# Where ScalarE rounds the fourth seam block's weights: ahead of or behind two low masks

## What is computed

```python
def ssd_chunked(x, dt, a, bm, cm):          # 4 chunks of 128 tokens, 4 groups of 8 heads
    ...
    a_cum = jnp.cumsum(a_dt, axis=-1)
    decay_mat = jnp.exp(segsum(a_dt))
    cb = jnp.einsum('bclgn,bcsgn->bgcls', cm, bm)
    y_diag = jnp.einsum('bgecls,bcsgep->bclgep', cb[:, :, None] * decay_mat, xdt)
    ...
    y_off = jnp.einsum('bclgn,bcgepn,bgecl->bclgep', cm, prev, jnp.exp(a_cum))
    return (y_diag + y_off).reshape(b, s, SSM_HEADS, SSM_HEAD_DIM)
```

## Time and profile before

| | us |
|---|---|
| median of 3 runs | 1220.28 (1220.24 to 1220.58) |
| the profiled execution, whole | 1220.1 |
| its span, first to last instruction | 1218.4 |
| TensorE busy in it | 1203.7 (99%) |
| VectorE busy | 856.1 (70%) |
| ScalarE busy | 641.1 (53%) |
| GpSimd busy | 88.6 (7%) |

### The profile page before, as it was taken

One profiled execution on the slowest core, in us unless ns is written; L12 is line 12 of the kernel. 1 busy time (PEld: TensorE's weight loads), 2 busy tenths in 40 slices (PEclk: granted clock), 3 DMA queues, 4 the chain that ended last, 5 costly groups with the idle time before them and its releaser, 6 DMA issues.

```text
span 1218.4 us, 16218 instructions
## 1 busy us (share of the span) xinstructions
PE 1203.7 (99%) x5941; PEld 1005.8 (83%) x5941; DVE 856.1 (70%) x1573; ACT 641.1 (53%) x1193; POOL 88.6 (7%) x78
## 2 busy tenths in 40 slices
PE   7999999999999999999999999999999999999998
PEld 6998888788878887888778888888888888888887
DVE  6426898999899989999684533334788888884321
ACT  5615787778786878587856533224422323232210
POOL 1000001400060003300120000000000000000000
PEclk9999999999999999999999999999999999999999
DMA  6712243135413432144319333343233333334240
GB/s 204 205 34 72 70 104 104 35 90 104 110 44 76 107 92 84 50 97 104 104 52 318 108 93 104 104 154 115 60 103 97 93 104 88 103 99 136 95 138 35
DMA packets 230149, 124.65 MB, mean 102 GB/s; under 512 B 85198, under 2 KB 209718, under 8 KB 230070
## 3 DMA queue, kind: packets, MB, share of 16 engines
q1 hardware_dynamic: 228167, 120.40, 35.5%
q10 hardware_dynamic: 1902, 3.21, 0.7%
HBM read 110.99 MB, written 12.58 MB: 101 GB/s over the span
## 4 chain that ended last, share of the span: by engine, by line
PE 88%; DVE 9%; issue 1%; ACT 1%; DMA 1%; DVEq 0%; SPq 0%; ACTq 0%
PE g L688 15%; PE g L689 15%; PE g L690 15%; PE g L751 4%; PE g L753 4%; PE g L752 4%; PE t L681 4%; PE s L888 3%; PE ob L904 3%; PE s L1049 2%; PE s L1050 2%; PE s L1051 2%; PE t L810 1%; PE g L1051 1%; PE t L1049 1%
## 5 line engine op out<-in xcount | busy, mean ns | idle before, releaser
L1122 ACT ACTIVATE w_high<-wraw 128x1024 fp32r<-128x1024 f32 x175 | 184.4, 1059 | 287.2 <-DMA wraw<-in_ffn_w_up 135.1
L1682 DVE TENSOR_TENSOR w_low<-wraw,w_high 128x1024 fp32r<-128x1024 f32 x174 | 219.1, 1262 | 124.5 <-ACT w_high L1122 122.0
L688 PE MATMUL g<-hT_hi,w_high 128*128 128x512 f32 x360 | 156.4, 434 | 1.2 <-DVE hT_lo L1688 1.2
L690 PE MATMUL g<-hT_hi,w_low 128*128 128x512 f32 x360 | 141.2, 392 | 0.0
L689 PE MATMUL g<-hT_lo,w_high 128*128 128x512 f32 x360 | 140.9, 391 | 0.0
L688 PE MATMUL g<-h2T_hi,w_high 128*128 128x512 f32 x352 | 137.5, 390 | 0.1
L690 PE MATMUL g<-h2T_hi,w_low 128*128 128x512 f32 x352 | 137.1, 390 | 0.0
L689 PE MATMUL g<-h2T_lo,w_high 128*128 128x512 f32 x352 | 137.1, 389 | 0.0
L751 PE MATMUL g<-w_high,hT_hi 128*128 128x512 f32 x224 | 95.3, 425 | 0.0
L753 PE MATMUL g<-w_high,hT_lo 128*128 128x512 f32 x224 | 88.4, 395 | 0.0
L752 PE MATMUL g<-w_low,hT_hi 128*128 128x512 f32 x224 | 87.8, 392 | 0.0
(11 more groups left out here) (354 smaller groups left out, 2517.7 us busy)
## 6 DMA issues: line engine op xcount, KB each, us to landing
wraw<-in_w_in SPq DMA_DIRECT2D x140, 256.0 KB, 3.1
wraw<-in_ffn_w_up SPq DMA_DIRECT2D x88, 256.0 KB, 3.2
wraw<-in_ffn_w_down SPq DMA_DIRECT2D x44, 256.0 KB, 3.0
wraw<-in_w_proj_b SPq DMA_DIRECT2D x32, 256.0 KB, 3.3
yT_lo<-spill SPq DMA_DIRECT2D x6, 1024.0 KB, 9.7
spill<-xraw SPq DMA_DIRECT2D x64, 64.0 KB, 2.6
xcx<-spill SPq DMA_DIRECT2D x8, 512.0 KB, 5.6
wraw<-in_w_proj_a SPq DMA_DIRECT2D x16, 256.0 KB, 3.3
```

The source lines that it names most:

```text
L688: nc.tensor.matmul(gb[par][:, :], w, hi, start=k == 0, stop=False)
L690: return nc.tensor.matmul(gb[par][:, :], wl, hi, start=False, stop=last)
L1122: nc.scalar.activation(whi[slot_of(u)][:, :, :], wraw[u % 2][:, :, :], ACT.Copy).then_inc(w_hi, 1)
L1682: V.tensor_tensor(wlo[slot_of(u)][:, :, :], wraw[u % 2][:, :, :], whi[slot_of(u)][:, :, :].bitcast(F32), ALU.subtract).then_inc(w_lo, 1)
```

## The change

ScalarE's list in each group's seam is reordered by one place: `hi(u0 + 13)`, one instruction of 128 x 1024, moves from ahead of `am_low(2)` and `am_low(3)`, four instructions of 128 x 128 each, to behind them. All else is the same.

```diff
@@ -1518,9 +1518,9 @@
                 state_high(1)
                 seg_e(1)
                 state_high(2)
-                hi(u0 + 13)
                 am_low(2)
                 am_low(3)
+                hi(u0 + 13)
                 evac_late(1)
                 for k in range(8):
                     if k < 6:
```

## The result

The changed kernel takes **1226.40 us** (median of 6 runs, 1225.48 to 1227.17) against 1220.36 for the kernel before (6 runs, 1220.24 to 1220.79): ratio 1.0049, 95% interval 1.0038 to 1.0059. It is slower by 6.0 us, where 2.4 were forecast and 1223.6 was the end of the range. The profiled run took 1227.11, with a span of 1225.4, 7.0 above that of before.

A forecast was written before the change was run, and what follows sets the result against it. TensorE, busy 99% of the span, was taken as the bound. Three groups at +0.88 us (2.65) less 0.30 in the last gave +2.35, so 1220.28 + 2.4 = 1222.7 us; 80% range 1219.9 to 1223.6.

The forecast's parts named there:

- The stall that the change removes: At seg(2), TensorE's wait for ScalarE's low mask goes whole, 0.84 us per group; the moved hi costs nothing.
- The gain waited away at `step(4)`: step(4) waits for masked(4), the end of a gapless VectorE row, so the direct 3.4 us gain is at best lost there.
- Three copies blocked, 0.20 lost at `step(2)`: Earlier GpSimd blocks three VectorE copies instead of two; masked(2) ends later and step(2) loses 0.20 us of the gain.
- The decisive turn: GpSimd's skip(2) comes 0.14 us ahead of VectorE's lo(u0+13) and takes its turn; step(4) +0.88 us in each of three groups.
- TensorE, full from there on, doesn't win it back: Behind step(4), VectorE catches up by masked(7), but TensorE keeps the delay: 3 x 0.88 = 2.65 us.
- a further turn is lost: Rival: in each group copies or 2103 lose another turn, about 1 us more; +5 to +6, 1225.8 us; 8%.

The follow-up runs named there:

- e1_turn: Changed kernel plus one wait per group: GpSimd's skip(2) also waits for masked(3), so that lo(u0+13) has its turn first; 1220.12 us.
- e5_late14: Changed kernel with the eight constant copies moved to the last attention unit (n = 7) and hi(u0+14) moved behind am_low(7) on ScalarE; 1216.85 us.
- e7_split: On top of e5_late14, the eight copies split in two halves, four at n = 6 and four at n = 7; 1216.47 us.
- e2_fill: Changed kernel with eight matmuls that nobody reads ahead of TensorE's wait at step(4) in groups 0 to 2; 1222.36 us.
- e4_stall: Kernel before, old order, with from_state(1) on VectorE repeating its first product once in group 0 and twice in group 1; 1224.68 us.

## Why the prediction was wrong

- **The stall that the change removes: right.** ScalarE's masks came 0.95 earlier and `seg(2)` 0.84, in all four groups, and the moved `hi` cost nothing.
- **The gain waited away at `step(4)`: right.** `e1_turn` shows it alone: 1220.12, with 0.96 us of idle time there instead of 0.36.
- **Three copies blocked, 0.20 lost at `step(2)`: right.** From `seg(2)` to `step(2)` TensorE's delay grows from 1.85 to 2.05.
- **The decisive turn: right.** The order and the margin of 0.14 us came out as worked out; `step(4)` moved by 0.89 to 0.91 against a forecast of 0.88, and the last group by -0.30, with `lo` keeping its turn by 0.04 us (621.69 against 621.73). That last one is partly luck: at 0.02 us the turn at 2122 went one way in `e5_late14` and the other in `e7_split`. Restoring the turn removes the cost (`e1_turn`). The Trainium skill's rule ("SBUF — State Buffer", Who interferes with whom) that the order of issue decides who blocks held here down to 0.14 us.
- **The step that failed** is the sentence "TensorE, full from there on, doesn't win it back": the stall was priced as the time that it takes. I foresaw a wait of some 2 us at `step(4)` and took a full clock behind it for granted, a term put at nothing without a reason. It fell to half for 3.41 us in each of three groups, 1.6 us each and 4.7 in all, twice the sum that I had. No rival held that. The earlier trace rows had waits of 0.65 and 0.36 us and a full clock behind both, and the longest inside the trace before, at the start-up, was 1.15. That bounded nothing for a wait of 1.8; a bound from above was owed. Without the half clock (`e2_fill`) the time is 1222.36, inside the range and 0.3 from the forecast.
- **The rival "a further turn is lost"** had nearly the right time (+5 to +6) for the wrong reason; the trace shows no such turn.

What stays open: from which idle time on the clock falls, and why it doesn't do so each time. The traces show it full behind 0.36 to 1.36 us and halved behind 1.8 (three times) and 2.36 (once). By the times and mean clocks of the runs without a trace, it can go either way behind waits like these: one run of `e4_stall` seems to have stayed full behind both of its waits, and one to have fallen behind both.

## What to carry to other kernels

When a change lets one engine run earlier, lay the engines that it releases on the same time axis: here GpSimd came 0.56 us earlier, took the turn of VectorE's `lo(u0+13)`, and 0.9 us lost on a 70% busy engine delayed the 99% busy one by 0.9. When the sum makes a wait of TensorE longer than those already in the trace, price the clock behind it as well, and ask whether something can fill the wait. Here a stall was worth removing only together with what was late next: the reorder alone cost 6.0 us, the copies' move alone gave nothing, and both with one more instruction out of the way gave 3.5.

## What the runs showed of the hardware

- A TensorE idle time of 1.8 us in an otherwise full stream was followed, 0.7 to 1.0 us after its end, by 3.41 us at half clock, with TensorE busy throughout them; the cost was 1.57 to 1.59 us each time. Idle times of 0.65, 0.79, 0.96 and 1.36 us had full clock behind them in the traces. By the runs' mean clocks, not every wait of 1.8 or 2.4 us was followed by a half clock.
- VectorE's instructions on two SBUF operands and GpSimd's take turns, and the pattern is exact enough to compute with: over a chain of some fifteen instructions it gave `step(4)` to 0.03 us. At margins of 0.14 and 0.04 us it said rightly who had the turn; at 0.02 us the turn went either way. A long instruction that misses its turn (1.22 to 2.07 us) ends 0.9 us later and shifts the row behind it by as much. The small copies of lines 1845 and 1847, with one SBUF operand, are held as well (0.92 to 1.03 us instead of 0.2). A VectorE instruction that reads PSUM is not held: line 2090 took 0.68 us beside `skip(2)` in the kernel before.
